# Products of the experts' output biases behind the first and the second step of the first expert

## The reference, cut to what matters

```python
def expert_block(j):
    ...
    hid = tokens[rows] @ w_exp_in[e] + b_exp_in[e]
    out = _clamped_swiglu(hid) @ w_exp_out[e] + b_exp_out[e]
    return out * wts[:, None].astype(out.dtype)
...
x = x + gate2 * _moe(h, ...)
return _rmsnorm(x, final_norm_w)
```

## Time and profile before

| | |
|---|---|
| median of three runs | 2703.44 us |
| the profiled execution: its own time | 2704.88 us |
| its span, first to last instruction | 2702.8 us |
| PE, PEld, DVE, ACT, POOL busy | 96%, 78%, 56%, 33%, 1% of the span |
| chain that ended last, by engine | PE 77%, DMA 11%, DVE 7%, ACT 3% |
| read from device memory | 699.43 MB, 260 GB/s over the span |
| mean granted clock of PE | 0.978 of 2.4 GHz |

### The profile page before, as it was taken

One profiled execution on the slowest core, in us unless ns is written; L12 is line 12 of the kernel. 1 busy time (PEld: TensorE's weight loads), 2 busy tenths in 40 slices (PEclk: granted clock), 3 DMA queues, 4 the chain that ended last, 5 costly groups with the idle time before them and its releaser, 6 DMA issues.

```text
span 2702.8 us, 47659 instructions
## 1 busy us (share of the span) xinstructions
PE 2588.1 (96%) x19460; PEld 2096.8 (78%) x19461; DVE 1513.5 (56%) x2701; ACT 898.4 (33%) x1388; POOL 36.7 (1%) x24
## 2 busy tenths in 40 slices
PE   7999999999999999999979978999999999999998
PEld 6999699999999969999968977965555555555554
DVE  5666666666766666666655786543444434334344
ACT  4344454444443445444433534411111111111111
POOL 0000000000000000000000110000000000000000
PEclk8999999999999989999989988999999999999999
DMA  9644544445455455544443323689999999999997
GB/s 266 232 178 166 211 179 179 157 181 186 164 186 186 164 214 195 187 163 179 176 158 140 117 76 145 233 344 425 430 430 429 431 430 430 430 429 431 430 430 307
DMA packets 70926, 704.62 MB, mean 261 GB/s; under 512 B 11063, under 2 KB 11319, under 8 KB 14343
## 3 DMA queue, kind: packets, MB, share of 16 engines
q1 hardware_dynamic: 65736, 695.11, 64.3%
q0 software_dynamic: 5088, 8.05, 1.4%
HBM read 699.43 MB, written 3.67 MB: 260 GB/s over the span
## 4 chain that ended last, share of the span: by engine, by line
PE 77%; DMA 11%; DVE 7%; ACT 3%; issue 1%; SPq 0%; DVEq 0%; ACTq 0%
PE ps L1628 15%; PE ps L1631 15%; PE ps L1632 15%; DMA slot<-in_experts 11%; PE ps L2140 10%; PE ps L2164 6%; PE ps L2120 4%; PE ps L2177 2%; DVE u_lo L981 2%; PE ps L1659 1%; PE ps L1663 1%; PE ps L1662 1%; PE ps L2150 1%; ACT u_hi L558 1%; ACT hs L581 1%
## 5 line engine op out<-in xcount | busy, mean ns | idle before, releaser
L981 DVE TENSOR_TENSOR u_lo<-ring,u_hi 128x1024 fp32r<-128x1024 f32 x500 | 616.1, 1237 | 464.0 <-ACT u_hi L558 460.5
L558 ACT ACTIVATE u_hi<-ring 128x1024 fp32r<-128x1024 f32 x498 | 523.9, 1057 | 692.6 <-PE ps L1628 641.0
L1628 PE MATMUL ps<-hs,u_hi 128*128 128x256 f32 x2408 | 693.7, 288 | 19.8 <-DVE hs L1007 17.4
L1631 PE MATMUL ps<-hs,u_hi 128*128 128x256 f32 x2408 | 687.1, 285 | 0.0
L1632 PE MATMUL ps<-hs,u_lo 128*128 128x256 f32 x2408 | 686.7, 285 | 0.0
L1628 PEld LDWEIGHTS ps<-hs,u_hi 128*128 128x128 f32 x2408 | 467.8, 194 | 31.4 <-issue 20.8
L1631 PEld LDWEIGHTS ps<-hs,u_hi 128*128 128x128 f32 x2408 | 468.3, 194 | 0.5
L1632 PEld LDWEIGHTS ps<-hs,u_lo 128*128 128x128 f32 x2408 | 468.1, 194 | 0.0
L2140 PE MATMUL ps<-slot,xg 128*64 128x256 f32 x4032 | 460.5, 380 | 5.6 <-DMA slot<-in_experts 5.6
L2140 PEld LDWEIGHTS ps<-slot,xg 128*64 128x64 f32 x4032 | 287.5, 137 | 210.9 <-issue 66.4
L2164 PE MATMUL ps<-slot,eact 128*64 128x512 f32 x1008 | 244.1, 605 | 0.0
(11 more groups left out here) (355 smaller groups left out, 3041.6 us busy)
## 6 DMA issues: line engine op xcount, KB each, us to landing
slot<-in_experts SPq DMA_DIRECT2D x248, 1536.0 KB, 18.8
ring<-in_stream SPq DMA_DIRECT2D x184, 1536.0 KB, 6.5
extra_in<-in_experts SPq DMA_DIRECT2D x4, 1024.0 KB, 11.9
slot<-in_experts SPq DMA_DIRECT2D x4, 1024.0 KB, 4.9
bias<-bias_rows POOLq DMA_DIRECT2D x2, 1280.0 KB, 12.6
konst<-in_konst POOLq DMA_DIRECT2D x1, 2272.0 KB, 15.0
extra_out<-in_experts SPq DMA_DIRECT2D x4, 512.0 KB, 9.5
slot<-in_experts SPq DMA_DIRECT2D x4, 512.0 KB, 15.1
```

Source lines behind the costliest of these rows:

```text
L558: nc.scalar.activation(u_hi[buffer_of(l, k)][:, :], raw_unit(l, k), ACT.Copy).then_inc(unit_hi, 1)
L981: nc.vector.tensor_tensor(u_lo[b][:, :], raw_unit(l, kk), u_hi[b][:, :].bitcast(F32), ALU.subtract).then_inc(unit_lo, 1)
L1628: mm = mm_(dst, hi, x_hi, start=first, stop=False, skip_group_check=True)
L1631: mm_(dst, hi, x_lo, start=False, stop=False, skip_group_check=True)
```

## The change

The four products are no longer made in one group ahead of the first `expert_in`. Two of them, for the first token block, are made behind step 0 of the first expert, and two, for the second block, behind its step 1, all through banks 6 and 7. DVE's adds stand behind its own steps 0 and 1 (`add_bias`). PE's waits for `wtT_taken` and `bout_scaled` go with the first pair, the second pair waits until the first has been added, the wait for `rows_taken` stays ahead of the first `expert_in`, and the wait for all four adds stands directly behind the second pair.

```diff
--- before.py
+++ after.py
@@ -274,7 +274,7 @@
 
         SSUM, DOWN = 2, 4
         SECOND_OUT = (0, 1, 6, 7)
-        BIAS_BANKS = (1, 3, 4, 7)
+        BIAS_BANKS = (6, 7)
         LAST_BANKS = ((6, 7), (2, 5))
 
         tile_landed = [sem(f"tile_landed{i}") for i in range(RING)]
@@ -1559,18 +1559,23 @@
             step(nc.vector.tensor_scalar(flagf[:, :], count_up[:, 0:PASSES - 1], float(CAP), fullest[:, 0:1], ALU.mult, ALU.is_lt))
             nc.vector.tensor_copy(flags[:, 1:PASSES], flagf[:, :]).then_inc(flags_ready, 1)
 
+            def add_bias(t):
+                for half in range(2):
+                    v.wait_ge(bias_sums_ready, 2 * t + half + 1)
+                    ys = y_tok[:, t, half * 512:half * 512 + 512]
+                    nc.vector.tensor_tensor(ys, ys, ps[:, BIAS_BANKS[half], :], ALU.add).then_inc(ybias_taken, 1)
+
             def expert_pass(p):
                 n = p * EXPERTS
                 take_tokens(p, 0, 0, after_first=False)
-                if isinstance(p, int):
-                    for i in range(2 * TT):
-                        v.wait_ge(bias_sums_ready, i + 1)
-                        ys = y_tok[:, i // 2, i % 2 * 512:i % 2 * 512 + 512]
-                        nc.vector.tensor_tensor(ys, ys, ps[:, BIAS_BANKS[i], :], ALU.add).then_inc(ybias_taken, 1)
                 v.wait_ge(placeT_ready, n + 1)
                 find_places(1)
                 expert_step(p, 0, 0, 0, after=False)
+                if isinstance(p, int):
+                    add_bias(0)
                 expert_step(p, 0, 1, 0, after=False)
+                if isinstance(p, int):
+                    add_bias(1)
                 with v.Fori(0, EXPERTS // 2 - 1) as e:
                     expert_turn(p, e * 2, 0)
                     expert_turn(p, e * 2 + 1, 1)
@@ -2198,14 +2203,16 @@
                 expert_step(p, e + 1, 0, 1 - b, last=last)
                 expert_step(p, e + 1, 1, 1 - b, last=last)
 
-            def bias_sums():
-
-                pe.wait_ge(wtT_taken, 1)
-                pe.wait_ge(bout_scaled, 1)
-                pe.wait_ge(rows_taken, 4)
-                for i in range(2 * TT):
-                    rows = slice(32 * i, 32 * i + EXPERTS)
-                    mm_(ps[:, BIAS_BANKS[i], :], wtT[rows, i // 2 * P:(i // 2 + 1) * P], bout[rows, i % 2 * 512:i % 2 * 512 + 512], start=True,
+            def bias_sums(t):
+
+                if t == 0:
+                    pe.wait_ge(wtT_taken, 1)
+                    pe.wait_ge(bout_scaled, 1)
+                else:
+                    pe.wait_ge(ybias_taken, 2 * t)
+                for half in range(2):
+                    rows = slice(32 * (2 * t + half), 32 * (2 * t + half) + EXPERTS)
+                    mm_(ps[:, BIAS_BANKS[half], :], wtT[rows, t * P:(t + 1) * P], bout[rows, half * 512:half * 512 + 512], start=True,
                         stop=True).then_inc(bias_sums_ready, 1)
 
             def expert_pass(p):
@@ -2214,13 +2221,17 @@
                     pe.wait_ge(scat_added, n * (2 * TT))
                 gather(n, first=True)
                 if isinstance(p, int):
-                    bias_sums()
+                    pe.wait_ge(rows_taken, 4)
                 expert_in(p, 0, 0, 0)
-                pe.wait_ge(ybias_taken, 2 * TT)
                 expert_in(p, 0, 1, 0)
                 turn(n, 0, first=True)
                 expert_step(p, 0, 0, 0, first=True)
+                if isinstance(p, int):
+                    bias_sums(0)
                 expert_step(p, 0, 1, 0, first=True)
+                if isinstance(p, int):
+                    bias_sums(1)
+                    pe.wait_ge(ybias_taken, 2 * TT)
                 expert_turn(p, 0, 0)
                 expert_turn(p, 1, 1)
                 with pe.Fori(1, EXPERTS // 2 - 1) as e:
```

## The result

Over twelve runs the changed kernel took 2709.73 us (2708.57 to 2712.21) and the kernel before 2703.93 (2702.03 to 2704.89), a ratio of 1.0023 with a 95% interval of 1.0015 to 1.0030: **5.8 us slower**. The forecast was 2708.2, 4.8 us slower.

The account below looks back on a forecast made before the run. PE's chain ahead of the last DMA pause was taken to set when the expert-weight stream, and so the kernel, ends. Terms 1.23 + 2.12 + 1.5 = 4.85 us on 2703.4 gave 2708.2 us, range 2703.5 to 2711.0.

Parts of the forecast that it names:

- that rival: Behind the second pair: idle PE also brings the clock down for 3.4 us; +6.5 us, 2710.0; chance 0.14.
- the border of 5.4: Whole run: 0.2%, 5.4 us, is what a measurement can tell from no change; the border is 2708.9 us.
- The bound: Expert pass: ends with the weight transfers; PE delays between 1764 and 1818 us delay the end by the same amount.
- Step 1: Ahead of the first `expert_in`: without the products it starts 0.9 us sooner, and 1.1 us of PE becomes idle.
- Step 2: First two `expert_in` groups: clock rises 3.4 us later, a loss of 1.23 us; other end a gain of 0.47.
- The rival "clock as before": First `expert_in` groups: clock rises at the same moment as in the old trace; +3.1 us, 2706.6; chance 0.26.
- Step 3: Behind steps 0 and 1 of the first expert: two pairs of products cost 2.12 us, ends 2.0 and 4.2.
- Step 4: Directly behind the second pair: PE idles 1.5 us waiting for DVE's adds, ends 1.28 and 1.9.
- Steps 5 and 6: DVE's adds stay covered by PE's work (up to 1.3 us otherwise); no DMA moved, early refills end before the pause.

Follow-up runs that it names:

- the second set: The changed kernel unchanged, run once more against the kernel before: 2710.47 against 2703.13 us, ratio 1.0026 (1.0016 to 1.0036).
- The filled hole: Changed kernel plus one product of constants in PE's idle time ahead of the first `expert_in`: 3.7 us over the kernel before, ratio 1.0012.

## Why the prediction was right, point by point

The direction and the range held, and so did the mechanism in all terms but one: behind the second pair the clock fell, which the forecast had left to a rival. By the traces the move is 6.82 us; that is nearer to that rival (+6.5, chance 0.14) than to the sum of 4.85. That the first set of runs came out at 5.8, only 1.0 us from the forecast, is in part luck: the second set had 7.3. Of the chances, 0.68 lay on "within 0.2%" and 0.30 on slower; 5.8 and 7.3 us lie past the border of 5.4, though the intervals reach below it. By its steps:

- **The bound.** PE ahead of the last DMA pause, the stream behind it. Right: 4.64 us of added work gave 4.7 us, and the distance from the first L482 issue to the end is the same in every profile within 0.9 us. Between the two first profiles the end moved 0.8 us more than the issue, which is inside that spread.
- **Step 1, the front.** `expert_in` starts at 1765.19 (forecast 1765.15), behind 1.13 us of idle time (1.1).
- **Step 2, the clock.** I took the later rise, 1770.8 and a loss of 1.23 us. Measured: 1770.7 and 1.27 (1775.07 against 1773.80), 1.26 in the kernel without products. The filled hole brings the rise back. The trace agrees with the rule cited from the Trainium skill (TensorE: Matmul & The Clock Gate, "What's actually happening"), that sustained activity releases the throttle: the clock stayed low behind the stretch with 2.17 of 3.30 us busy and rose behind the one with 3.30 of 3.30. The rival "clock as before" is out: in all seven profiles that have the hole unfilled the two groups take 9.84 to 9.91 us.
- **Step 3, two pairs.** 2.12 forecast; 1.06 + 1.11 in the chain. A price I had not seen comes with each pair: the `expert_in` group behind it takes 3.60 instead of 3.45 us, 0.15 more (behind the second pair in the kernel without the wait). It is the same 3.60 that the group behind a `turn` takes (1775.44); the cause was not tried.
- **Step 4, the wait.** 1.5 forecast, 1.32 measured (1794.40 less 1793.08). I had DVE start 0.13 us behind the pair; its first add needs only the pair's first product and started at 1793.06, before the pair was done.
- **The step that was too small** is the price of that wait. I had put the fall of the clock behind it into a rival with a chance of 0.14, at 1.7 us, since the stretch from 1654.7 to 1658.1 showed PE half idle with no fall. It came in all three profiles and cost 1.76 us (5.36 less 3.60), close to that rival's 1.7. That is most of the miss; the forecast had it at nothing. Whether it comes depends on where the idle time lies: with the hole filled it did not.
- **Steps 5 and 6.** DVE's adds and step stayed under their cover; the first pair's adds ended at 1783.66, and `turn` for step 2, which needs DVE's step 1, came behind a gather that began at 1785.94.

The sum with the measured terms is 1.27 + 1.06 + 1.11 + 0.30 (0.15 behind each pair) + 1.32 + 1.76 = 6.82 us, the whole move of the first L482 issue. The forecast of 4.85 lacks the fall (1.76) and the 0.30; its other terms miss by 0.2 or less.

## What to carry to other kernels

Work that fills an engine's wait is cheaper than its duration: the products took 2.02 us of PE in the old place and cost 0.9 of wall time, and as PE was busy with them the clock rose earlier, so that leaving them out made this part 1.3 us longer; in the new place they cost 2.5 us (2.17 and twice 0.15) and drew a wait and a low clock behind them. Before a group is moved, ask what wait it covered, what clock it ran at and which banks let it run as one, and where in the program time is bought at all: ahead of the last pause of the transfers each microsecond of PE counted whole, behind it four products were free. A wait belongs ahead of the first instruction that needs it, here behind the next group of matmuls, and not directly behind the work it waits for.

## What the runs showed of the hardware that I had not expected

- Four products of 32 rows, each on 32 partitions and in a bank of its own, took 1.07 us at 2.4 GHz, two of them 1.06 to 1.11: two more were free.
- A kernel with less work (no products) took 1.3 us longer from the first gather to the first L482 issue.
